# Half of GpSimd's bias additions moved behind the first layer's key transfers, and the sixteen transfers of a head split nine to seven

## The reference, cut to what matters

```
# first layer, per head (16 heads of 128), in chunks of 32 positions
b = cumsum(log f);  b_last = b at the chunk's end
o     = causal(q_dec k_inv^T) v + q_dec state
state = exp(b_last) * state + (k * exp(b_last - b))^T v      # keys decayed to the chunk's end
# second layer, per head and group of (window, dilation)
s = q k^T * E**-0.5 + bias_table[t5_bucket(distance)]
o = softmax(s) v
```

## Time and profile before

| | before |
|---|---|
| median of 3 runs | 1585.5 us (1585.32 to 1586.35) |
| profiled execution | 1585.65 us, its span 1583.9 us |
| PE busy | 1575.3 us, 99% of the span |
| DVE, ACT, POOL busy | 813.3, 628.4, 417.2 us |
| granted TensorE clock | 1.00 in all of the span |

### The profile page before, as it was taken

One profiled execution on the slowest core, in us unless ns is written; L12 is line 12 of the kernel. 1 busy time (PEld: TensorE's weight loads), 2 busy tenths in 40 slices (PEclk: granted clock), 3 DMA queues, 4 the chain that ended last, 5 costly groups with the idle time before them and its releaser, 6 DMA issues.

```text
span 1583.9 us, 23925 instructions
## 1 busy us (share of the span) xinstructions
PE 1575.3 (99%) x8611; PEld 1304.4 (82%) x8611; DVE 813.3 (51%) x1439; ACT 628.4 (40%) x1066; POOL 417.2 (26%) x790
## 2 busy tenths in 40 slices
PE   9999999999999999999999999999999999999998
PEld 8788888888887888888888888888888888888887
DVE  7784685586577733444333444433345441434445
ACT  6453453454354533333232333332343332233333
POOL 5621122122100092222173211248022225502210
PEclk9999999999999999999999999999999999999999
DMA  6334323333621354444344443435344433534421
GB/s 194 108 90 123 84 89 111 84 89 113 185 80 46 123 145 105 105 104 116 87 144 110 117 96 94 104 95 164 91 104 109 115 84 127 146 90 110 109 73 67
DMA packets 281990, 171.63 MB, mean 108 GB/s; under 512 B 72320, under 2 KB 254672, under 8 KB 281904
## 3 DMA queue, kind: packets, MB, share of 16 engines
q1 hardware_dynamic: 215200, 139.93, 31.6%
q0 software_dynamic: 24560, 29.42, 6.3%
q10 hardware_dynamic: 42144, 1.05, 1.5%
HBM read 144.37 MB, written 5.71 MB: 95 GB/s over the span
## 4 chain that ended last, share of the span: by engine, by line
PE 95%; DVE 1%; POOL 1%; ACT 1%; issue 0%; DMA 0%; ACTq 0%; POOLq 0%
PE proj L566 82%; PE inner L566 3%; PE inner L947 2%; PE inner L942 2%; PE inner L900 1%; PE inner L881 1%; PE inner L814 1%; POOL qk L476 1%; PE inner L817 1%; PE inner L803 1%; PE inner L779 1%; PE inner L896 0%; POOL kT L307 0%; PE inner L824 0%; PE inner L825 0%
## 5 line engine op out<-in xcount | busy, mean ns | idle before, releaser
L1390 DVE TENSOR_TENSOR w_lo<-raw,w_hi 128x1024 fp32r<-128x1024 f32 x252 | 307.4, 1221 | 465.7 <-ACT w_hi L994 462.6
L566 PE MATMUL proj<-u_hi,w_hi 128*128 128x512 f32 x1280 | 505.9, 395 | 0.0
L566 PE MATMUL proj<-u_lo,w_hi 128*128 128x512 f32 x1280 | 499.0, 390 | 0.0
L566 PE MATMUL proj<-u_hi,w_lo 128*128 128x512 f32 x1280 | 498.8, 390 | 0.0
L994 ACT ACTIVATE w_hi<-raw 128x1024 fp32r<-128x1024 f32 x252 | 265.3, 1054 | 190.0 <-PE proj L566 128.9
L566 PEld LDWEIGHTS proj<-u_hi,w_hi 128*128 128x128 f32 x1280 | 240.4, 188 | 53.4 <-issue 4.0
L566 PEld LDWEIGHTS proj<-u_hi,w_lo 128*128 128x128 f32 x1280 | 240.3, 188 | 51.5
L566 PEld LDWEIGHTS proj<-u_lo,w_hi 128*128 128x128 f32 x1280 | 240.5, 188 | 48.1
L540 POOL DMA_DIRECT2D rows<-qx x240 | 118.0, 500 | 254.6 <-DVE qx L1818 252.7
L566 PE MATMUL proj<-w_hi,u_hi 128*128 128x512 f32 x440 | 173.7, 395 | 0.0
L566 PE MATMUL proj<-w_hi,u_lo 128*128 128x512 f32 x440 | 171.4, 390 | 0.0
(11 more groups left out here) (220 smaller groups left out, 1729.7 us busy)
## 6 DMA issues: line engine op xcount, KB each, us to landing
raw<-at_w_in SPq DMA_DIRECT2D x160, 512.0 KB, 4.3
raw<-hg_w_in SPq DMA_DIRECT2D x63, 512.0 KB, 4.1
rows<-qx POOLq DMA_DIRECT2D x240, 44.0 KB, 2.5
raw<-hg_w_out SPq DMA_DIRECT2D x16, 512.0 KB, 3.6
raw<-at_w_out SPq DMA_DIRECT2D x16, 512.0 KB, 4.8
v<-rows POOLq DMA_DIRECT2D x64, 64.0 KB, 2.3
v<-qk POOLq DMA_DIRECT2D x192, 16.0 KB, 3.2
v<-x SPq DMA_DIRECT2D x4, 512.0 KB, 6.1
```

The costliest lines, as they stand in the source:

```text
L566: ins = nc.tensor.matmul(bank[:, :], stationary(a), moving(b), start=(first and n == 0), stop=(last and n == 2))
L1390: nc.vector.tensor_tensor(w["lo"][:, slot, :], raw[:, slot, :], w["hi"][:, slot, :].bitcast(F32), ALU.subtract).then_inc(w_ready, 1)
```

## The change

The first 27 additions and `turn_chunks(None)` stay where they are. The other 28 additions are executed by POOL behind the loop of quads and the last quad, in front of the table's store; `ext_ready` is signalled by the last of them as before. The sixteen strips become one list in the order of the destination strip; POOL issues the first nine, SP the last seven, and the two signals that PE waits for count 144 and 112 a head in place of 128 each.

```
--- before.py
+++ after.py
@@ -300,12 +300,13 @@
         def square_of(transfer):
             return tmp[:, 0, :] if transfer else enb[:, :]
 
-        def move_strips(eng, to, moved):
-
-            for c in to:
-                for i in range(NC):
-                    eng.dma_start(kT[c * CH:(c + 1) * CH, :, i * CH:(i + 1) * CH],
-                                  turned_keys[i * CH:(i + 1) * CH, c, :, :]).then_inc(moved, 16)
+        STRIPS = [(c, i) for c in range(NC) for i in range(NC)]
+        BY_POOL = 9
+        def move_strips(eng, strips, moved):
+
+            for c, i in strips:
+                eng.dma_start(kT[c * CH:(c + 1) * CH, :, i * CH:(i + 1) * CH],
+                              turned_keys[i * CH:(i + 1) * CH, c, :, :]).then_inc(moved, 16)
 
         def own_keys(g):
             return g - (H - HQ) + 1
@@ -430,7 +431,7 @@
                         h = (n - SLOTS) // HG.per_head
                         if layer is HG and n - SLOTS == h * HG.per_head and 0 <= h < HQ and by_transfer(last):
                             wait_turn(sp, sp_met, keys_turned, head(q, h) + 1)
-                            move_strips(sp, range(NC // 2, NC), keys_high)
+                            move_strips(sp, STRIPS[BY_POOL:], keys_high)
                 quads(sp, body)
 
             sp.wait_ge(O_done, 2 * H)
@@ -468,19 +469,21 @@
                                        staged_hg[(NC - 1 - c) * CH:(NC - c) * CH, s // 2, :]).then_inc(v_turned[s // 2], 16)
 
             runs = list(bias_runs())
-            for n, (g, bucket, first, count) in enumerate(runs):
-
-                if n == len(runs) // 2:
-                    turn_chunks(None)
-                run = slice(g * EXT + first, g * EXT + first + count)
-                ins = nc.gpsimd.tensor_scalar(ext_sb[:, run], ext_sb[:, run],
-                                              relb_sb[:, bucket * GROUPS + g:bucket * GROUPS + g + 1], None, ALU.add)
-            ins.then_inc(ext_ready, 1)
+            def add_bias(some):
+
+                for g, bucket, first, count in some:
+                    run = slice(g * EXT + first, g * EXT + first + count)
+                    ins = nc.gpsimd.tensor_scalar(ext_sb[:, run], ext_sb[:, run],
+                                                  relb_sb[:, bucket * GROUPS + g:bucket * GROUPS + g + 1], None, ALU.add)
+                return ins
+
+            add_bias(runs[:len(runs) // 2])
+            turn_chunks(None)
 
             def move_keys(q, h):
 
                 wait_turn(pool, pool_met, keys_turned, head(q, h) + 1)
-                move_strips(pool, range(NC // 2), keys_low)
+                move_strips(pool, STRIPS[:BY_POOL], keys_low)
 
             def hg_body(q, last):
                 for h in range(HQ):
@@ -490,6 +493,7 @@
                     turn_chunks(q)
             quads(pool, hg_body)
 
+            add_bias(runs[len(runs) // 2:]).then_inc(ext_ready, 1)
             pool.wait_ge(ext_ready, 1)
             pool.dma_start(ext_dram.rearrange("g h e -> h g e"),
                            ext_sb.rearrange("h (g e) -> h g e", g=GROUPS)).then_inc(ext_stored, 16)
@@ -795,8 +799,8 @@
                     for turned in v_turned:
                         pe.wait_ge(turned, (g // HQ + 1) * 16 * NC)
                 if transfer:
-                    pe.wait_ge(keys_low, 8 * NC * NC * (g + 1))
-                    pe.wait_ge(keys_high, 8 * NC * NC * (g + 1))
+                    pe.wait_ge(keys_low, 16 * BY_POOL * (g + 1))
+                    pe.wait_ge(keys_high, 16 * (len(STRIPS) - BY_POOL) * (g + 1))
                 else:
                     pe.wait_ge(kT_ready, own_keys(g))
                 for b in range(ST - 1):
```

## The result

| | before | changed |
|---|---|---|
| median | 1585.41 us (1585.2 to 1586.35, 4 runs) | 1604.93 us (1602.99 to 1605.1, 4 runs) |
| ratio to before | 1 | 1.0119 [1.0102, 1.0137] |
| profiled execution, span | 1585.65, 1583.9 us | 1605.1, 1603.4 us |
| PE busy | 1575.3 us | 1580.4 us |
| PE's wait at `updates` | 1.3 us, 1 head | 15.6 us, 11 heads |

A forecast was written before the change was run, and what follows sets the result against it. PE, busy 99% of the span, was taken to bound the kernel; head 0's wait would shrink by 0.25 us and all other terms count nothing, so 1585.5 - 0.25, rounded 1585.3 us, range 1584.4 to 1586.3.

The forecast's parts named there:

- the first of the signs: PE's wait at `updates`: the forecast is wrong if PE waits in several heads; no head but head 0 should wait.
- What bounds the kernel: PE, busy 99% of the span; of its waits only the 1.3 us at `updates` in head 0 belongs to the change.
- Part 1: Head 0, additions gone: POOL's first strip begins at 56.07, a gain of 0.67 us.
- Part 2: Head 0, nine strips: POOL's ninth issued at 60.38 or up to 0.28 later, landing at 62.21; SP's share 0.65 us shorter.
- Part 3: PE's wait in two steps: the register operation adds 0.05 us in head 0 (0 to 0.1), nothing in the other eleven.
- Head 0's sum: `updates` begins at 62.30 instead of 62.56, 0.25 us earlier (nothing to 0.54 gained); the wait shrinks to about 1.1.
- Part 5: Behind the loop: the moved additions are hidden by POOL's 142.71 us wait for ACT; SP's earlier weight loads give nothing.
- The landing range: POOL's strips land 1.6 to 2.0 us after issue; head 0's ninth between 61.98 and 62.38.
- Part 4: The other eleven heads: a cover of 0.2 to 0.6 us hides the later ninth strip; nothing lost, at worst 0.3 us.
- The rivals: SP's landing sets the end, 1584.5 us, chance 0.10; nothing gained, 1585.5, 0.15; POOL's issues held up by DVE, 1590, 0.04.
- The one of a held-up POOL: All heads with transfers: POOL's issues wait for DVE's operations, nine ending 0.84 us later; 1590 us, chance 0.04.
- the 0.02 that was left for something unseen: Chance of 0.02 kept for an outcome outside the forecast (0.69) and its three rivals; no size given.

The follow-up runs named there:

- e3: The changed kernel, with SP waiting until POOL's nine strips have landed before it issues the next weight load; 1586.54 us, ratio 1.0004.
- e1: The kernel before with only the additions moved behind the loop, strips left at eight and eight; 1585.35 us, ratio 0.9996.
- e9: The changed kernel with 20 tiny POOL transfers added behind the values' transfers of each of the first three quads; 1601.9 us, ratio 1.0102.
- e4: The changed kernel with one more strip-sized SP transfer, into an unused tile, between its seven strips and the weight load; 1591.06 us, ratio 1.0031.
- e7: e4 with 20 tiny POOL transfers added behind the values' transfers of each of the first three quads; 1585.28 us, ratio 0.9996.
- e2: The kernel before with only the split of nine and seven strips, additions left in front of the loop; 1607.22 us, ratio 1.0135.
- e8: e1 with three strip-sized POOL transfers into an unused tile ahead of POOL's eight strips in each head; 1626.13 us, ratio 1.0251.
- e6: e4 with 34 tiny POOL transfers added at the very start of the program; 1591.28 us, ratio 1.0028.
- e5: The changed kernel with the split turned round, seven strips by POOL and nine by SP; 1585.62 us, ratio 0.9994.

## Why the prediction was wrong

PE waits in several heads, which is the first of the signs that the prediction itself named for being wrong.

**Right.**
- What bounds the kernel, and where it would show: PE alone, and its wait at `updates`.
- Part 1: POOL's first strip in head 0 was put at 56.07; it begins at 55.98.
- The issues of Part 2: the ninth at 60.29, against 60.38; SP's share 4.61 us, against the 5.26 of the earlier trace rows, shorter by exactly the spacing of 0.65.
- Part 3: PE goes on 0.12 us behind the landing, where 0.09 was taken. In e3 it is 0.12 as well.
- Head 0's sum, as long as the collision is away: in e3 the landing is 62.05 and `updates` begins at 62.17; 62.21 and 62.30 were forecast, with a wait of 1.0 to 1.2, and e3's is 0.94.
- Part 5's additions: hidden, as e1 shows by itself. They begin at 409.78, since the loop itself ends later, and take 10.08 us there, not the 15.64 of the earlier trace rows.

**The step that failed** is the last sentence of Part 5: SP is free 0.65 us sooner in front of the next weight loads, PE waits for none of these, "so this gives nothing either". I asked who waits for the load, found nobody, and wrote zero. I did not ask what the load would run into. It brings 512 KB onto the DMA engines that have to carry the strip on which PE does wait, and the same change puts that strip 0.54 us later. Both shifts stand in the prediction, 0.65 in Part 2 and 0.54 beside it, as a gain here and a cost there; they were never laid on one time axis. In place of that zero the runs show the whole loss: with the load moved away it is gone (e3, 1586.54 us), and the collision costs 16.3 us without the hold (e9). The margin could have been read from the trace of before: head 0's last strip at 60.80, and the load behind SP's eight (55.52 + 5.26 = 60.78) issued at 61.15, in the row of before above. Afterwards the load comes at 61.15 - 0.65 = 60.50, and the ninth strip at the 60.38 of Part 2: a margin of 0.12, where 0.06 was measured. In the other heads the margins of 1.10 to 1.29 shrink by 1.19, to between -0.09 and 0.10; -0.06 to 0.11 was measured, but for head 11 with its hold. Head 1, with 1.62, is left 0.43 (measured 0.36), and is the one that doesn't wait.

**The landing range** of Part 2 follows from that. The 1.6 to 2.0 us of the earlier trace rows are 96 transfers that were all issued 0.35 us or more ahead of the load; none of them was issued level with a load or behind it, so they could not bound the ninth. The range was good for the place where it was measured, and the strip was moved out of that place. A row that could have warned was in my own list: the weight load that took 14.3 us in the midst of the table's spreading. I used it for Part 5 and not here.

**Part 4** fell with it. Its cover of 0.2 to 0.6 us was even too small: in head 8 the strip issued at 318.44 would have landed near 320.09 and did so at 322.00, and PE waited only 0.46, so some 1.5 us were covered; in head 9 it was 0.9 (1.69 late, 0.78 waited). A landing that is 1.6 to 3.0 us later than it should be breaks a cover of that size all the same.

**What was not priced.** The clock: 3.0 us in the two heads with the longest waits. And the hold: the earlier trace rows show 2.90 us of POOL with no releaser, and I read this row for another purpose without asking whether twelve more strips would move it onto the path.

**The rivals.** None of the three took place; what came falls to the 0.02 that was left for something unseen. The one of a held-up POOL (1590) has the right side and the wrong place: POOL's nine issues take 4.86 us, as 8 x 0.54 + 0.55 makes it, and none but those of head 1 (5.03, with 0.18 between two of them) and of head 11 (6.78, with the hold) took over 4.89. The Trainium skill has a sentence that would have led there: DMA: Bandwidth & Descriptors, section Issuing engines are not separate DMA queues, says that transfers started by different engines run on the same 16 DMA engines and interleave. The trace agrees with the first half (in the changed kernel POOL's last strip takes 3.2 to 4.7 us where SP's load is issued level with it or ahead, and 1.67 where the load comes 0.36 us later). Of the interleaving, the Trainium skill says in the same page's section Queues, rings and completion order that an engine takes packets from its queues in turn. In 61.4 to 62.5 us no packet of POOL's moved while SP's queue used 46.7% of the engines. So taking turns at the packets does not by itself explain the first 1.1 us; where the strip stood in that time the profile does not show, and no run here settles it.

## What to carry to other kernels

When a change makes a queue free sooner, find what that queue issues next and what it will share the DMA engines with; a large load that nobody waits for can still push aside the small transfer on which everything waits. Write the issue times of both queues on one axis, before and after, and look at the margin between the last small transfer and the next large one; here 0.24 us or more kept it whole and 0.16 or less did not. If work has to be rebalanced between two queues, put something small in front of the large load (e4, e7), or let the load wait for the small transfer (e3), rather than hand the freed time to the load.

## What the runs showed of the hardware

- **A short transfer beside a long one.** A strip of 12 KB, issued by POOL, lands 1.6 to 2.2 us after its issue when SP's load of 512 KB is issued 0.24 us or more behind it (the closest, with 0.245 in e2, 0.246 in e9 and 0.27 in e8: 1.63, 1.66 and 1.66). With margins from 0.16 down to -2.67 it takes 3.0 to 4.9 us. Between 0.16 and 0.24 there is one value, 2.40 us at 0.23 (e8).
- **A hold at POOL's 129th transfer**, counted from its first addition, in ten of the eleven kernels: it begins 1.8 to 3.2 us late and waits for nothing that the profile shows: 2.90 at the store of the table before, 3.21 there in e1, 1.88 to 1.90 in a strip of after, e2, e3, e4 and e6, 2.39 in a strip of e8, 1.79 and 1.76 at a tiny transfer in e7 and e9. Extra transfers in the loop moved it (e7, e8, e9), extra ones ahead of the first addition did not (e6). In e5 a hold of 0.85 stands at the 125th. What it is stays open.
- **The clock** fell to 1.2 GHz for a part of the stretch behind waits of 2.73 and 3.06 us of PE, and did not behind one of 2.08 (0.77, 0.74 and 1.00 above). The length of the wait alone doesn't decide: in e8 it fell in head 2 behind 2.01 us and in head 6 behind 1.88, and in head 4 it did not behind 1.88. The rows of heads 2 and 4:

```profile
113.34:119.00 5.66, 5.66 (x23) 4.90 (x24) 3.81 (x7) 1.31 (x3) 0.00 (x0) 0.70 0.08 26
202.54:209.00 6.46, 6.46 (x38) 5.72 (x39) 4.21 (x7) 2.61 (x5) 0.00 (x0) 1.00 0.10 29
```

- **POOL's additions:** the same 28 took 15.64 us in front of the loop and 10.08 behind it. Why is not shown.
